# Encoder layer, one core: real-valued position transform inside the second projection, channel transform inside w_in, turned x kept in DRAM, no set-up block

## The chip, the cores and the metric

The kernel runs on one core of one Trainium2 chip. The metric is the device time of one execution in microseconds (us). The kernel before took 4788.79 us, median of three runs (4778.67 to 4791.86). The execution whose trace is read here took 4788.77 us, with a span of 4787.0 us from its first to its last instruction.

## The reference, cut to what matters

One encoder layer is applied to two sequences of 4096 and 2048 positions, 6144 rows of 1024 channels together, all in float32. One projection of RMSNorm(x) gives the queries, keys and values of 12 heads, two gates, and the 256 channels `u` of a Fourier branch:

```
h = rmsnorm(x, norm_g)
proj = h @ w_in
q, k, v, g_attn, u, g_four = split(proj)
q, k = rmsnorm per head
attn = merge of three dilated windowed attentions * silu(g_attn)
uf = u.reshape(B, S, 4, 64)
mixed = fftn(uf, axes=(1, 3), norm="ortho").real
four = einsum('bsgc,gce->bsge', mixed, w_four) * silu(g_four)
return x + concat[attn, four] @ w_out
```

`mixed` is the real part of a two-dimensional transform over the positions and the 64 channels of a group. `w_four` follows as a 64 x 64 matrix for each group. Since `u` is real, the spectrum over the channels of a group is symmetric: 33 cosine and 31 sine sums hold all of it.

## The kernel before, in words

Engines are programmed with semaphores; each engine and each DMA queue works its own list in order, and a block ends when all of its engines have ended. The rows are worked in 48 tiles of 128. There are six blocks, one after the other.

**setup** (L162) loads the constants, multiplies a one-hot table with `rel_bias` (L199, four products into `line`) and folds `w_four` into the channel transform (L203, into `chan_w`).

**project** (L218) runs twice. In each run 1792 columns of `w_in` come in 16 units through six staging buffers (L329); ScalarE rounds each unit into `w_hi` (L476) and VectorE takes the rest into `w_lo` (L596), so that a product of float32 values is three products of rounded ones (L381). A tile has four banks of results, `ps[0]` to `ps[3]`, in the order 3, 0, 1, 2: three of 512 columns and bank 3 of 256, so 72 products of 512 columns and 24 of 256. Ahead of them x is loaded (L318), normalised (`norm_x`), turned by eight TensorE transposes (`turn`, L368, between bank 3 and bank 0, for the next tile) and split into `h_hi` (L431) and `h_lo` (L527). The first run gives q, k and u. Its u is turned by two more transposes (L388) and multiplied by `chan_w` (L396), and 512 columns per row go to the scratch `ab`. Its GpSimd queue fills the pads of `v` (L302) and then spreads `line` into `skew` tables, DRAM to DRAM, by 36 DMAs (L311). The second run loads and turns x again with the kept `rstd_x`, and gives v and the two gates; a gate's silu is an exponential on ScalarE (L454) and three operations on VectorE (L556, L558, L564). Both runs go over the tiles in a hardware loop. The end of the second run issues the first loads of the next block (L335 and L636).

**fourier** (L638) does the transform over the positions in two levels, with float32 matrices. Level 1 multiplies by the 64- or 32-point matrix (L726), cosine and sine halves stacked, and stores the scratches `g_a` and `g_b`; level 2 multiplies by the fine matrices (L731) and stores `four`. All its loads and stores are on SyncE's queue (L636, L683, L695), in pieces of 4096 columns; ScalarE and VectorE copy the results out (L744).

**attention** and **combine** follow. Attention begins with loads of q, k, v and `skew`; combine reads `four` and the gates, and multiplies by `w_out` (L1349).

Of the kernel before, what the change touches and what calls it, by code (L numbers as in the profile page):

```python
# [55 lines left out]
PIECE = 8 * BANK  # L56
# [32 lines left out]
def constants():  # L89
# [7 lines left out]
    a = 2 * np.pi * np.outer(np.arange(HD), np.arange(HD)) / HD  # L97
    two = np.eye(2)
    chan = np.concatenate([np.kron(two, np.cos(a)), np.kron(two, np.sin(a))], axis=1)
    out = {"c_ident": np.eye(P), "c_onehot": onehot, "c_chan": chan}  # L100
    for name, s in zip("ab", SEQS):
        n1 = s // N2
        a = 2 * np.pi * np.outer(np.arange(n1), np.arange(n1)) / n1
        c, sn = np.cos(a), np.sin(a)
        out["c_first_" + name] = np.block([[c, -sn], [-sn, -c]])
        n, k1, k2 = np.arange(N2)[:, None, None], np.arange(n1)[None, :, None], np.arange(N2)[None, None, :]
        a = 2 * np.pi * ((n * (k1 + n1 * k2)) % s) / s
        second = np.concatenate([np.cos(a), np.sin(a)], axis=0) / math.sqrt(s * HD)
        out["c_second_" + name] = second.reshape(2 * N2, n1 * N2)
# [19 lines left out]
def build(nc, io):  # L129
    core = Core(nc, io)  # L130
    with core.keep:
        core.ident = core.sb(core.keep, "ident", [P, P])
        core.rstd_x = core.sb(core.keep, "rstd_x", [P, TILES])
        scratch = {"q": [TOKENS, DA], "k": [TOKENS, DA], "v": [TOKENS + 2 * VPAD, VROW], "gate": [TOKENS, D],
                   "ab": [TOKENS, 2 * DF], "four": [TOKENS, DF], "line": [NH, TABLE],
                   "o": [len(DILS), TOKENS, OROW],
                   "g_a": [2 * SEQS[0] // N2, N2 * DF], "g_b": [2 * SEQS[1] // N2, N2 * DF]}
        scratch |= {f"skew{x.dil}": [NH, x.copies] for x in SPREADS}
        core.dram = {k: nc.dram_tensor("scratch_" + k, s, F32, kind="Internal").ap() for k, s in scratch.items()}
        with ExitStack() as tables:  # L140
            core.zero = core.sb(tables, "zero", [P, VW])
            core.chan_w = core.sb(tables, "chan_w", [P, 2, 2 * P])
            core.line = core.sb(tables, "line", [NH, TABLE])
            setup(core)
            project(core, 0)

        with ExitStack() as spectrum:
            core.four_in = core.sb(spectrum, "four_in0", [P, PIECE])
            core.four_first = {n: core.sb(spectrum, "four_first_" + n, [2 * seq // N2, 2 * seq // N2])
                               for n, seq in zip("ab", SEQS)}  # L150
            core.four_in_loaded, core.four_table_in = core.sem("four_loaded0"), core.sem("four_table_in")
            project(core, 1)
            fourier(core)
# [8 lines left out]
def setup(core):  # L162

    nc, io, dram = core.nc, core.io, core.dram
    loaded, cleared, mm_done = (core.sem("setup_" + n) for n in ("loaded", "cleared", "mm_done"))
    with ExitStack() as st:
        onehot = core.sb(st, "onehot", [BUCKETS + 1, TABLE])
        rel = core.sb(st, "rel", [BUCKETS + 1, NH])
        line = core.line
        chan = core.sb(st, "chan", [P, 2 * P])  # L170
        wf = core.sb(st, "wf", [P, 2, P])
        ps_line = [core.ps(st, f"ps_line{i}") for i in range(-(-TABLE // BANK))]
        ps_chan = [core.ps(st, f"ps_chan{i}") for i in range(2)]
        block = st.enter_context(nc.Block())
        n_loads = 4 + NG

        @block.gpsimd
        def _(pool):
            pool.memset(wf[:], 0.0).then_inc(cleared, 1)
            pool.memset(rel[:], 1.0).then_inc(cleared, 1)  # L180
            pool.memset(core.zero[:], 0.0).then_inc(cleared, 1)

        @block.sync
        def _(sp):
            sp.dma_start(core.ident[:], io["c_ident"]).then_inc(loaded, 16)
            sp.dma_start(onehot[:], io["c_onehot"]).then_inc(loaded, 16)
            sp.dma_start(chan[:], io["c_chan"]).then_inc(loaded, 16)
            sp.wait_ge(cleared, 3)
            sp.dma_start(rel[0:BUCKETS, :], io["rel_bias"]).then_inc(loaded, 16)
            for g in range(NG):  # L190
                lo = HD * (g % 2)
                sp.dma_start(wf[lo:lo + HD, g // 2, lo:lo + HD], io["w_four"][g]).then_inc(loaded, 16)

        @block.tensor
        def _(pe):
            pe.wait_ge(loaded, 16 * n_loads)
            for i in range(len(ps_line)):
                n = min(BANK, TABLE - i * BANK)
                pe.matmul(ps_line[i][0:NH, 0:n], rel[:], onehot[:, i * BANK:i * BANK + n],  # L199
                          start=True, stop=True).then_inc(mm_done, 1)  # L200
            for gp in range(2):
                for ab in range(2):
                    pe.matmul(ps_chan[gp][:, ab * P:(ab + 1) * P], chan[:, ab * P:(ab + 1) * P], wf[:, gp, :],  # L203
                              start=True, stop=True).then_inc(mm_done, 1)

        @block.vector
        def _(dve):
            dve.wait_ge(mm_done, len(ps_line) + 2 * 2)
# [3 lines left out]
            for gp in range(2):  # L212
                dve.tensor_copy(core.chan_w[:, gp, :], ps_chan[gp][:, 0:2 * P])
# [392 lines left out]

class Piece:  # L610


# [874 lines left out]
```

## Time and profile before

| | |
|---|---|
| median of three runs | 4788.79 us (4778.67 to 4791.86) |
| profiled execution, its own time | 4788.77 us |
| its span | 4787.0 us |
| TensorE busy | 4527.7 us (95%) |
| VectorE busy | 2811.1 us (59%) |
| ScalarE busy | 1744.2 us (36%) |
| GpSimd busy | 749.8 us (16%) |
| mean DMA rate | 115 GB/s |

The profile page gives busy time by engine for the whole span, and then the span in 40 slices. Since the blocks follow each other, a block's own length is read from where SyncE issues the first DMA of the next block, and what bounds it is read from the rows of that stretch alone. Matmuls are pipelined: the cost of one is the distance from its start to the start of the next, not its own duration.

### The profile page before, as it was taken

How to read it: one execution, taken by the hardware profiler on the slowest of the kernel's cores; microseconds unless marked ns; L12 is line 12 of the kernel's file. 1: busy time of each engine (PE TensorE's matmuls, PEld its weight loads, DVE VectorE, ACT ScalarE, POOL GpSimd, SP SyncE). 2: the span in 40 equal slices, each digit the busy share in tenths (PEclk: the TensorE clock that was granted, in tenths of full speed). 3: DMA queues.
4: the chain of work that ended last, by engine and by line, in shares of the span. 5: the costliest groups of instructions: out<-in, count | busy, mean ns of one | idle time of the engine just before them, and what ended most of it. 6: DMA issues, size and time to landing. Idle time of an engine off the chain costs nothing. (4 is left out here: it accounts for less than half of the span.)

```text
span 4787.0 us, 86571 instructions
## 1 busy us (share of the span) xinstructions
PE 4527.7 (95%) x28848; PEld 3805.0 (79%) x28848; DVE 2811.1 (59%) x8424; ACT 1744.2 (36%) x4667; POOL 749.8 (16%) x1494
## 2 busy tenths in 40 slices
PE   3999999998999999998499999999999999899999
PEld 2888888886888888873397988979889798778887
DVE  2555555555655555652265656647566466577776
ACT  2222222223222222211254655546555465533332
POOL 2000000000000000000042433424344243300000
PEclk9999999999999999997799999999999999999999
DMA  7212121214211222219833434434353343466665
GB/s 185 79 66 79 66 79 66 78 73 138 74 69 67 74 74 74 74 61 255 183 101 81 120 87 117 102 81 118 87 119 102 81 118 79 133 234 239 243 241 191
DMA packets 549470, 549.16 MB, mean 115 GB/s; under 512 B 187432, under 2 KB 443304, under 8 KB 547797
## 3 DMA queue, kind: packets, MB, share of 16 engines
q1 hardware_dynamic: 502228, 474.35, 34.1%
q0 software_dynamic: 46976, 71.46, 5.3%
q8 instruction: 144, 2.36, 0.2%
q14 instruction: 122, 0.99, 0.1%
HBM read 344.66 MB, written 211.33 MB: 116 GB/s over the span
## 5 line engine op out<-in xcount | busy, mean ns | idle before, releaser
L381 PE MATMUL p_ps<-p_w_hi,p_h_hi 128*128 128x512 f32 (+1 forms) x3072 | 1155.1, 376 | 55.2 <-DVE p_w_lo L596 49.4
L381 PE MATMUL p_ps<-p_w_hi,p_h_lo 128*128 128x512 f32 (+1 forms) x3072 | 1133.2, 369 | 0.0
L381 PE MATMUL p_ps<-p_w_lo,p_h_hi 128*128 128x512 f32 (+1 forms) x3072 | 1133.0, 369 | 0.0
L1167 ACT ACTIVATE att_p<-att_s_b,att_o 128x256 f32<-128x256 f32 (+2 forms) x1728 | 739.2, 475 | 815.8 <-DVE att_o L1217 792.8
L1112 PE MATMUL att_ps_o<-att_v,att_p_t 128*128 128x130 f32 (+1 forms) x6528 | 943.4, 288 | 46.3 <-DMA att_v<-scratch_v 32.9
L1112 PEld LDWEIGHTS att_ps_o<-att_v,att_p_t 128*128 128x128 f32 (+1 forms) x6528 | 817.1, 192 | 146.8 <-issue 47.8
L381 PEld LDWEIGHTS p_ps<-p_w_hi,p_h_hi 128*128 128x128 f32 x3072 | 582.9, 190 | 162.6 <-DVE p_w_lo L596 46.6
L1035 POOL DMA_DIRECT2D scratch_o<-att_o x864 | 503.5, 587 | 1069.3 <-DVE att_o L1224 1047.6
L381 PEld LDWEIGHTS p_ps<-p_w_hi,p_h_lo 128*128 128x128 f32 x3072 | 583.1, 190 | 104.7
L381 PEld LDWEIGHTS p_ps<-p_w_lo,p_h_hi 128*128 128x128 f32 x3072 | 583.2, 190 | 101.7
L1217 DVE CUSTOM_DVE_ANT_0 att_s_b<-att_ps_s,att_bias 128x256 f32<-128x256 f32 (+2 forms) x1488 | 500.0, 386 | 54.1 <-PE att_ps_s L1084 46.9
L1098 PE MATMUL att_ps_p<-ident,att_p 128*128 128x128 f32 (+1 forms) x3264 | 455.8, 282 | 0.0
L1224 DVE COPY att_o<-att_ps_o 128x260 f32<-128x260 f32 x432 | 184.0, 426 | 435.5 <-PE att_ps_o L1112 434.2
L1098 PEld LDWEIGHTS att_ps_p<-ident,att_p 128*128 128x128 f32 (+1 forms) x3264 | 349.1, 139 | 56.3 <-issue 18.5
L558 DVE RECIPROCAL p_denom<-p_denom 128x256 f32<-128x256 f32 x144 | 329.2, 2286 | 4.9
L431 ACT ACTIVATE p_h_hi<-p_ps_t,p_gain 128x128 fp32r<-128x128 f32 x768 | 208.4, 382 | 208.9 <-PE p_ps_t L368 208.9
L538 DVE TENSOR_REDUCE p_sumsq<-p_squares 128x8 f32<-128x512 f32 x144 | 98.7, 686 | 312.7 <-ACT p_squares L437 312.7
L556 DVE TENSOR_SCALAR p_denom<-p_expo 128x256 f32<-128x256 f32 x144 | 48.1, 334 | 387.8 <-ACT p_expo L454 387.8
L437 ACT ACTIVATE p_squares<-p_ps 128x512 f32<-128x512 f32 x144 | 86.1, 598 | 475.3 <-PE p_ps L381 475.3
L1137 ACT ACTIVATE att_p_t<-att_ps_p 128x512 f32<-128x512 f32 (+2 forms) x528 | 243.1, 478 | 0.8 <-PE att_ps_p L1098 0.2
L527 DVE SCALAR_TENSOR_TENSOR p_h_lo<-p_ps_t,p_gain,p_h_hi 128x128 fp32r<-128x128 f32 x768 | 206.8, 342 | 32.6 <-ACT p_h_hi L431 32.6
L1140 DVE COPY att_p_t<-att_ps_p 128x512 f32<-128x512 f32 x288 | 197.5, 686 | 4.0 <-PE att_ps_p L1098 3.4
(158 smaller groups left out, 5930.5 us busy)
## 6 DMA issues: line engine op xcount, KB each, us to landing
att_v<-scratch_v SPq DMA_DIRECT2D x1056, 65.0 KB
scratch_o<-att_o POOLq DMA_DIRECT2D x864, 66.0 KB, 2.7
out_o<-scratch_o SPq DMA_DIRECT2D x144, 396.0 KB, 5.5
p_x<-x SPq DMA_DIRECT2D x96, 512.0 KB, 4.5
scratch_gate<-p_gate SPq DMA_DIRECT2D x48, 512.0 KB, 3.5
out_gate<-scratch_gate SPq DMA_DIRECT2D x48, 512.0 KB, 6.3
out_x<-x SPq DMA_DIRECT2D x48, 512.0 KB, 4.9
y<-out_y SPq DMA_DIRECT2D x48, 512.0 KB, 3.0
```

What stands on the lines that cost most here:

```text
L381: ins = pe.matmul(ps[c][:, 0:width[c]], a[s][:, k, :], b[:, k, cols], start=(k == 0 and n == 0), stop=(k == KC - 1 and n == 2))
L431: ins = act.activation(h_hi[s][:, 4 * j + k, :], ps_t[2 * s + j][:, k * P:(k + 1) * P], ACT.Copy, scale=gain[:, 4 * j + k:4 * j + k + 1])
L527: ins = dve.scalar_tensor_tensor(h_lo[s][:, kk, :], ps_t[2 * s + j][:, k * P:(k + 1) * P], gain[:, kk:kk + 1], h_hi[s][:, kk, :].bitcast(F32),
L558: dve.reciprocal(denom[:, w], denom[:, w]).then_inc(chain, 1)
L1035: pool.dma_start(to, o[u % O][:, t, :]).then_inc(stored[u % O], 16)
L1098: ins = pe.transpose(ps_p[t][0:n, (2 * e + j) * P:(2 * e + j + 1) * P], p[u % 2][:, t, e, first:first + n], core.ident[:])
L1112: ins = pe.matmul(ps_o[:, col:col + 2 * VW], p_t[u % 2][0:n, t, e, j, :], v[u % V][0:n, unit.chunk(at, part), e * VW:(e + 2) * VW], start= ...
L1137: copy = (lambda to, src: engine.activation(to, src, ACT.Copy)) if t == 0 else engine.tensor_copy
L1140: copy(p_t[u % 2][:, t], src).then_inc(p_copied[t], 1)
L1167: act.activation(p[u % 2][:, t, e, 0:at.w], s_b[u % 2][:, t, e, 0:at.w], ACT.Exp, bias=o[u % O][:, t, PAIR_V + e:PAIR_V + e + 1], scale=-1 ...
L1217: dve.tensor_tensor_reduce(at.view(s_b[u % 2][:, t, e, :]), at.view(ps_s[2 * t + e][:, 0:2 * P]), at.bias(bias[b][:, e, :]), -1.0, -3 * NE ...
L1224: dve.tensor_copy(o[u % O][:, :, 0:PAIR_V], ps_o[:, 0:2 * PAIR_V].rearrange("p (t c) -> p t c", t=2)).then_inc(o_copied, 1)
```

## The change

There is no set-up block, and no Fourier block. What they did stands in the two projections, which are now two functions.

`project_first` turns the 256 columns of `w_in` that make u, multiplies them by a 64-point real channel matrix (`turn_w` and `mix_w`: 16 transposes and 16 float32 products of 128 columns), and splits the outcome into `w_hi` and `w_lo`. So the projection gives the channel spectrum itself, 256 real columns, and `turn_u` and `channel_dft` go. Banks run in the order 0, 1, 2, 3. It also stores each tile's `h_hi` and `h_lo` to a new scratch `ht`, 1 MB a tile, behind the load of x on SyncE's queue; the next write of the same buffer waits for that store.

`project_second` loads `h_hi` and `h_lo` from `ht` in place of x: no normalising, no turning, no splitting. Its tile loop is written out, not a hardware loop. Ahead of tile 1 it makes `line` and four small `mix` matrices (four one-hot products and eight float32 products), then the GpSimd queue issues the pads, two loads, and the 36 `skew` DMAs. From tile 3 on, TensorE runs one of 76 jobs behind the first 512-column bank and one behind the last bank of a tile, until tile 40: 24 `first` (two float32 products of 264 and 248 columns), 26 `second` (four of 128 columns, fewer in the last groups) and 26 `mix` (four of 128 columns). ScalarE copies each result out behind its gate work. The loads and stores of the jobs are on the GpSimd queue. The fine tables (3.2 MB) are loaded on SyncE's queue once the weights are split, into the space of the staging buffers.

Cut to its core, the diff is:

```diff
-            setup(core)
-            project(core, 0)
-            project(core, 1)
-            fourier(core)
+        project_first(core)
+        project_second(core)
...
+            def turn_w(r):
+                pe.wait_ge(w_in[r], 16)
...
+                        ins = pe.transpose(ps[2 + r % 2][:, at:at + P], stage[r][:, k, j * P:(j + 1) * P], core.ident[:])
...
+            def mix_w(r):
+                pe.wait_ge(u_copied, r + 1)
...
+                    ins = pe.matmul(ps_t[2 + r % 2][:, i * P:(i + 1) * P], u_t[r % 2][:, i * P:(i + 1) * P], chan[:],
+                                    start=True, stop=True)
...
-                    if half == 0 and n == (3 if first(t) else 1):
-                        turn_u(t)
-                    if half == 0 and n == (3 if first(t) else 2):
-                        channel_dft(t)
...
+                sp.wait_ge(lo_done, t * 2 + 2)
+                sp.dma_start(dram["ht"][bass.ds(t * HT, P), :],
+                             h_hi[s][:].rearrange("p k c -> p (k c)").bitcast(F32)).then_inc(h_stored[s], 16)
+                sp.dma_start(dram["ht"][bass.ds(t * HT + P, P), :],
+                             h_lo[s][:].rearrange("p k c -> p (k c)").bitcast(F32)).then_inc(h_stored[s], 16)
...
+            def load_h(t):
+                s = t % 2
+                if t >= 2:
+                    sp.wait_ge(mm_done[order[-1]], t - 1)
+                for part, to in enumerate((h_hi, h_lo)):
+                    row = t * HT + part * P
...
+            load_h(1)
+            sp.wait_ge(line_copied, LINES)
+            sp.dma_start(dram["line"], line[0:NH, 0:TABLE]).then_inc(line_out, 16)
+            sp.wait_ge(w_lo_done, len(units))
+            for wave in WAVES:
+                at = table_at[wave.name]
+                sp.dma_start(shared[:, at:at + (wave.slots + 1) * P], io["c_second_" + wave.name]).then_inc(table_in, 16)
+            for t in range(TILES):
+                s = t % 2
+                if t + 2 < TILES:
+                    load_h(t + 2)
...
+            load_first(0)
+            load_first(1)
+            pool.wait_ge(line_out, 16)
+            for at, x in zip(TABLE_AT, SPREADS):
...
+                    pool.dma_start(to, src).then_inc(skew_out, 16)
+            for nr in range(n_pieces):
+                store_first(nr)
+                if nr + 2 < n_pieces:
+                    load_first(nr + 2)
+            for s in range(2):
+                pool.wait_ge(g_stored[s], 16 * (n_pieces // 2))
+            load_second(0)
+            load_second(1)
...
+            for t in range(1, TILES):
...
+                for n, c in enumerate(order):
+                    if n == 0:
+                        pe.wait_ge(h_in[t % 2], 32 * (t // 2 + 1))
+                    product(t, c)
+                    if (t, n) in job_at:
+                        work(job_at[t, n])
```

## Rows read from the trace of the kernel before

**Rows 1.** The profile page: span, TensorE's busy time, clock granted in 40 slices.

```profile
span 4787.0 us, 86571 instructions
...
PE 4527.7 (95%) x28848; PEld 3805.0 (79%) x28848; DVE 2811.1 (59%) x8424; ACT 1744.2 (36%) x4667; POOL 749.8 (16%) x1494
...

```

**Rows 2.** By block: start:end, length, busy PE PEld DVE ACT POOL, clock, DMA, GB/s.

```profile
0.00:17.66 17.66, 8.05 (x16) 2.73 (x16) 2.83 (x6) 0.00 (x0) 0.65 (x7) 1.00 0.11 28
17.66:1142.21 1124.55, 1054.19 (x5280) 883.93 (x5280) 607.46 (x2032) 297.31 (x834) 25.65 (x41) 0.99 0.26 85
1142.21:2154.20 1011.99, 989.01 (x4992) 830.63 (x4992) 595.43 (x880) 222.63 (x641) 1.54 (x2) 0.99 0.24 80
2154.20:2339.64 185.44, 131.60 (x320) 55.61 (x320) 37.11 (x56) 31.76 (x56) 0.00 (x0) 0.77 1.03 244
2339.64:4787.00 2447.36, 2344.89 (x18240) 2032.12 (x18240) 1568.23 (x5450) 1192.53 (x3136) 721.98 (x1445) 0.97 0.48 134
```

**Rows 3.** TensorE by time between second projection and Fourier: start, length, line, idle before.

```profile
2144.29 0.40 PE L381 MATMUL p_ps<-p_w_hi,p_h_lo 128*128 128x512 f32 x1
2154.38 6.03 PE L726 MATMUL four_ps<-four_in,four_first_a 128*128 128x512 f32 x10 [9.69 <-PEq L270]
```

**Rows 4.** TensorE by time, one steady tile of the second projection.

```profile
1919.75 0.28 PE L381 MATMUL p_ps<-p_w_hi,p_h_hi 128*128 128x256 f32 x1
...
1922.60 1.04 PE L368 MATMUL p_ps_t<-ident,p_h 128*128 128x128 f32 x8
...
1923.70 0.39 PE L381 MATMUL p_ps<-p_w_lo,p_h_hi 128*128 128x512 f32 x1
...
1940.27 0.28 PE L381 MATMUL p_ps<-p_w_hi,p_h_hi 128*128 128x256 f32 x1
```

**Rows 5.** SyncE's stores of q, two tiles apart, in the first projection.

```profile
901.43 0.33 SPq L345 DMA_DIRECT2D scratch_q<-p_qk  x1
...
944.61 0.33 SPq L345 DMA_DIRECT2D scratch_q<-p_qk  x1
```

**Rows 6.** TensorE by time: the channel transform inside a steady tile.

```profile
1106.82 1.02 PE L396 MATMUL p_ps<-chan_w,p_ut 128*128 128x256 f32 x4
...
1107.91 0.40 PE L381 MATMUL p_ps<-p_w_lo,p_h_hi 128*128 128x512 f32 x1
```

**Rows 7.** TensorE by time: the first projection's longest early wait, and where tile 1 starts.

```profile
51.34 0.58 PE L381 MATMUL p_ps<-p_w_hi,p_h_hi 128*128 128x256 f32 x1 [15.86 <-DVE p_w_lo L596]
...
117.91 0.55 PE L381 MATMUL p_ps<-p_w_hi,p_h_hi 128*128 128x256 f32 x1 [2.37 <-DVE p_ab L585]
```

**Rows 8.** Columns as in rows 2: three stretches, loading weights with and without skew copies.

```profile
30.00:45.00 15.00, 1.62 (x6) 1.35 (x6) 2.85 (x9) 1.96 (x7) 13.32 (x23) 1.00 1.08 105
...
80.00:105.00 25.00, 15.90 (x48) 11.71 (x48) 9.62 (x8) 8.86 (x9) 0.00 (x0) 0.86 1.01 298
1157.00:1168.00 11.00, 11.00 (x53) 9.11 (x53) 8.68 (x8) 7.43 (x7) 0.00 (x0) 0.99 1.05 381
```

**Rows 9.** DMA issues from 18 to 130 us: count, KB each, median us to landing.

```profile
p_x<-x SPq DMA_DIRECT2D x3, 512.0 KB, 20.8
```

**Rows 10.** TensorE by time: 16 small float32 products in attention.

```profile
2388.03 1.95 PE L1112 MATMUL att_ps_o<-att_v,att_p_t 128*128 128x130 f32 x16
```

**Rows 11.** TensorE by time: the second projection's start, tile 0 and tile 1.

```profile
1152.10 0.55 PE L381 MATMUL p_ps<-p_w_hi,p_h_hi 128*128 128x256 f32 x1 [3.34 <-DVE p_w_lo L596]
...
1179.51 0.36 PE L381 MATMUL p_ps<-p_w_hi,p_h_hi 128*128 128x256 f32 x1 [3.50 <-DVE p_gate L564]
```

**Rows 12.** TensorE by time: the one-hot products in the set-up.

```profile
6.48 6.04 PE L199 MATMUL ps_line<-onehot,rel 33*12 33x512 f32 x8 [6.48 <-DMA wf<-w_four]
```

**Rows 13.** DMA issues of the whole span: count, KB each, median us to landing.

```profile
scratch_o<-att_o POOLq DMA_DIRECT2D x864, 66.0 KB, 2.7
...
four_in<-scratch_g_a SPq DMA_DIRECT2D x8, 1024.0 KB, 19.9
```

More of the change, by code:

```diff
@@ L55 @@
 N2 = 64
-PIECE = 8 * BANK
+COS = HD + 2
 def t5_bucket(rel):
@@ L103, in constants @@
         a = 2 * np.pi * np.outer(np.arange(n1), np.arange(n1)) / n1
         c, sn = np.cos(a), np.sin(a)
[L105 to L109, printed above, removed]
+        copies = np.eye(P // n1)
@@ L157, in build, with project_first @@
         combine(core)
[L162 removed]
+U_COLS = slice(3 * BANK, 3 * BANK + DF)
+HT = 2 * P
+def project_first(core):
     nc, io, dram = core.nc, core.io, core.dram
[L165 to L208, printed above, removed]
[L209 to L213 removed]
@@ new lines, in _, with __init__ @@
+            copy_u(3)
+            split_u(2)
+            split_u(3)
+            split(0, 0)
+            for n in range(PARTS, len(units)):
+                if n == 2 * PARTS + 2:
+                    norm_x(1, 1, X_LINKS)
+                split_w(n)
+            tiles(dve, step)
+class Wave:
+    def __init__(self, name, seq, base):
+        self.name, self.seq, self.base = name, seq, base
+        self.n1 = seq // N2
+        self.copies = P // self.n1
+        self.pieces = N2 // self.copies // 4
+        self.slots = self.n1 // 2
+        self.groups = [list(range(k, min(k + 4, self.slots))) for k in range(1, self.slots, 4)] + [[0]]
@@ new lines, with __init__, wave_jobs @@
+WAVES = [Wave(*at) for at in zip("ab", SEQS, BASES)]
+class Job:
+    def __init__(self, kind, wave, piece, part, slots=()):
+        self.kind, self.wave, self.piece, self.part, self.slots = kind, wave, piece, part, slots
+def wave_jobs():
+    jobs, nr, groups = [], 0, []
+    for wave in WAVES:
+        for i in range(wave.pieces):
+            jobs += [Job("first", wave, (nr, i), part) for part in range(2)]
+            nr += 1
+    for wave in WAVES:
+        groups += [(wave, slots) for slots in wave.groups]
+    mixes = lambda n: ([Job("mix", groups[n][0], n, i, groups[n][1][i:i + 2]) for i in range(0, len(groups[n][1]), 2)])
+    for n, (wave, slots) in enumerate(groups):
+        jobs += [Job("second", wave, n, j, slots) for j in ([0] if slots == [0] else [0, 1])]
+        if n >= 1:
+            jobs += mixes(n - 1)
+    return jobs + mixes(len(groups) - 1), groups, nr
```

757 lines of the change are left out of this document (459 added, 298 removed).

## The prediction, made before the result was known

> **What bounds the kernel now.** I read the page first, then the blocks one by one, then single tiles. The page says that TensorE is busy for 95% of the span and that its granted clock is low only in slices 18 and 19 [rows 1]. By block [rows 2]: set-up 17.7 us, first projection 1124.6, second 1012.0, Fourier 185.4, attention with combine 2447.4. In the Fourier block the DMA share is 1.03 and TensorE is busy for 131.6 of 185.4 us at a mean clock of 0.77: that block is bound by transfers, while in both projections the DMA share is about 0.25. So there is room beside the projections for what the Fourier block moves, if TensorE can take its products.
>
> In a steady tile of the second projection TensorE has no gap; the tile takes 1940.27 - 1919.75 = 20.52 us [rows 4], in the first projection 43.18 / 2 = 21.59 us [rows 5]. Here every instruction taken from TensorE is time gained, and every one added is time lost. The starts are another matter: in the first projection TensorE waits for weights, once for 15.9 us, and tile 1 starts only at 117.91, which is 100.3 us after its block began [rows 7]; in the second it starts at 1179.51, after 37.3 us [rows 11]. The difference is what the DMA engines do meanwhile: between 30 and 45 us, with pads and skew copies in flight, they are full and move 105 GB/s, later, with the skew copies, 298, and in the second start, without them, 381 [rows 8].
>
> **Fourier block and set-up.** Both blocks vanish. From where SyncE begins the Fourier block to where it begins attention is 185.4 us [rows 2], and the hand-over that remains (last product at 2144.29, next block's at 2154.38 [rows 3]) is counted with the projection. The set-up's 17.7 us go as well: the first projection's queue starts near 0.7 us.
>
> **First projection, steady tiles.** Two transposes and four products of 256 columns leave each tile. The four take 1107.91 - 1106.82 = 1.09 us less the 0.23 of the product between, 0.86 [rows 6]. All together are the difference between the two projections' tiles, 21.59 - 20.52 = 1.07 us [rows 4, 5]. So a tile is 20.52 us, bound by TensorE as in the second projection now. The new stores to `ht` add 1 MB a tile, 51 GB/s on a queue whose block mean is 85 of at least 298 [rows 2, 8]: hidden, and each has a whole tile before its buffer is written again. They stand behind the load of x and ahead of the stores of q, k and `ab`, which have that tile too.
>
> **First projection, start.** The skew copies and pads leave this stretch, the weight fold enters it. I walk it from the block's start: the first 256-column unit is in SBUF by 6 us; TensorE turns it, VectorE copies, TensorE multiplies, ScalarE and VectorE split, four rounds whose TensorE part is about 3 us each at the low pace of a cold start, so the fold ends near 20 us. The turning of x and its split follow (6 us), the first product stands at about 26 us. From there 12 units of 6 products, at 0.233 us (71 of them from 1923.70 to 1940.27 [rows 4]), make 16.8 us, the cold pace of the first ones and a wait of about 2 us for the second x make 4, and bank 3 is 2.9: tile 1 starts near 49.5 us. The weights no longer decide, since without skew copies they come at 381 GB/s [rows 8], a 0.5 MB unit in 1.4 us. Bounds: 42 us if the fold's rounds overlap fully; 100 us if the start stays as slow as it was [rows 7]. I take 49.5, near the second projection's 37.3 [rows 11] plus the fold. Then 47 tiles, the last without transposes: 49.5 + 47 x 20.52 - 0.9 = 1013; hand-over 7. The second block starts at 1020 instead of 1142.2, **122 us earlier**: 17 of the set-up, 51 of the tiles, 54 of the start.
>
> **Second projection, steady tiles.** Eight transposes go. They and the slower first product behind them reach from 1922.60 to 1923.70, 1.10 us, less 0.23 for the product, 0.87 [rows 4]: a tile is 19.65 us. VectorE and ScalarE lose the splits and the norm. The jobs come back to TensorE. A `first` job has 512 columns in float32, as many as the two channel products of 256: 0.86 us [rows 6]. `second` and `mix` jobs have 8 instructions of 128 columns, at 1.95 / 16 = 0.122 us each [rows 10] 0.98 us; the short groups less. Sum: 24 x 0.86 + 52 x 0.95 = 70 us. Bounds: 65 (all at the 0.86), and 148 (1.95 for each), if changing between the two kinds of products drained the array each time; rows 6 show such a change inside a tile without that loss, so I take 70. Their waits (results copied out three jobs before, pieces loaded two pieces before) lie a tile or more back: hidden by 20 us of products. Without that cover a piece would show a store and a load, 2 x 2.7 us [rows 13] or more. ScalarE's added copies come behind its gate work and have the next tile before their bank is needed.
>
> **Second projection, start.** h comes from DRAM, so the first product comes about 2 us sooner than 1152.10. Eleven small loads amid the weights cost about as much. So tile 0 ends about 32 us from the block's start, an estimate from rows 11 (37.3 less the 3.5 of the wait there, less 2). Then come the one-hot products, 6.04 us at the cold pace [rows 12], 3.0 warm; a wait for VectorE, which has the last gate and two copies ahead, 3.8 us (it is the 3.50 of rows 11, later); and 16 instructions of the small matrices, 2.0. Tile 1 starts at 40.8, was 37.3.
>
> **What the moved DMAs do there.** SyncE now queues the 3.2 MB of fine tables ahead of the h of tile 2, while pads and skew copies fill the GpSimd queue. Needed is that h at the end of tile 1, 60.5 us after the block's start. How the two queues share is shown for the first start alone: an x of 0.5 MB then took 20.8 us to land [rows 9], 25 GB/s. Between that and all of the 298 GB/s of rows 8 I take half, 149. 4.2 MB at 149 GB/s, from about 41 us, is there after 28 us, at 69; with 60 GB/s during the pads' last 10 us it is 72. The stall is 8 to 12 us; I take 11. Bounds: nothing (381 GB/s, all for SyncE), and 52 us (nothing until skew is done). The skew copies last some 100 us from tile 0's end, and the second pair of pieces behind them is needed about 10 us later: nothing, up to 30. Between the last `first` and the first `second` job lie a copy-out, a store and a load, by estimate some 12 us (two landings of 2.7 to 4, issues, the copy) against 9.5 of products: 3 us once. The Trainium skill, "DMA: Bandwidth & Descriptors", Queues, rings and completion order, says that an engine goes round the queues packet by packet; by that rule each queue gets about half, which is 149 here and a stall of 8 us, and the slow x of rows 9 disagrees in part. The skill's "SBUF — State Buffer", section on the DVE-blocks-DMA trap, speaks against moving DMAs to the GpSimd queue: VectorE's copies can hold up the writing of their descriptors. No row here shows it; it would add a few us to the 3.
>
> Block length to attention's start: 40.8 + 11 + 3 + 47 x 19.65 + 70 + hand-over 9.9 = 1058, against 1012.0: **46 us longer**.
>
> **Sum.** 1020 + 1058 + 2447 = 4525 us of span; with the 1.8 outside it (4788.77 less 4787.0) **4527 us**. The profiled execution is at the median of the runs (4788.77 and 4788.79), so nothing is to be shifted. A difference of 0.3%, 14 us, is about what a measurement of this kernel can tell from none.
>
> **The rivals.** First, the moved copies starve the second projection: SyncE gets nothing until the skew copies are done, h of tile 2 comes 52 us late instead of 11, pieces wait 20 more: 4527 + 61 = 4588. For it: the x that took 20.8 us. Against: rows 8, where weights still came beside skew. Second, the start of the first projection does not shorten, because the fold's chain takes the place of the skew wait: 4527 + 51 = 4578. Against it: 37.3 us without skew. Third, **slower than before**: the jobs stand in TensorE's own list, so each waits in place; if round trips on the GpSimd queue were as in the full Fourier block, where a load took 19.9 us [rows 13], and no tile hid them, store and load of each of 26 pieces and groups would cost 40 us, 26 x 40 = 1040. It decides from 262 / 26 = 10.1 us uncovered a piece; then the time is 4789 and above, at 12 us 4839. Against: the DMA share of 0.25, where 2.7 us is the landing. Fourth, that the copies disturb nothing and the fold overlaps: 4527 - 11 - 7 = 4509.
>
> **Chances.** Forecast 0.62, first rival 0.17, second 0.08, third 0.03, fourth 0.10. The forecast's own range is 4510 to 4555; with the fourth and most of the first two, **4500 to 4590**. Faster by over 0.3%: 0.96; within 0.3%: 0.01; slower: 0.03.
>
> **What would show it.** Attention should start at 2078 instead of 2339.64, with its own length unchanged. Tiles of 20.5 us in the first projection and 19.65 plus two jobs in the second; tile 1 of the first near 50 us; one wait for h at tile 2 of the second and one before the first `second` job, none longer than 15 us. Wrong would be: waits of TensorE for pieces in most tiles, a job far above 1 us, or tile 1 of the first projection after 70 us.

## The result, and the profile after

The changed kernel takes 4523.57 us, median of four runs (4521.0 to 4526.32); the kernel before, beside it, 4790.32 (4778.67 to 4796.84). The ratio is 0.9448, with a 95% interval of 0.943 to 0.9466: 267 us or 5.5% faster. The prediction was 4527, from 4500 to 4590. The profiled execution took 4521.0 us, with a span of 4519.2, 1.8 us outside it as before.

The page of the changed kernel, with the clock line of the page before ahead of it: TensorE is busy for 96%, and the dip that the Fourier block made in its clock (the two slices with a 7; 0.77 in [rows 2]) is gone.

```profile
PEclk9999999999999999997799999999999999999999
```

```profile
span 4519.2 us, 84021 instructions
...
PE 4347.2 (96%) x28408; PEld 3725.0 (82%) x28408; DVE 2586.4 (57%) x7796; ACT 1672.6 (37%) x4375; POOL 824.7 (18%) x1596
...
PEclk9999999998999999998999999999999999899999
```

By block, with the columns of [rows 2]: first projection, second projection, attention with combine.

```profile
0.00:1013.02 1013.02, 995.40 (x5040) 835.01 (x5040) 544.79 (x1892) 310.11 (x882) 0.21 (x5) 1.00 0.36 126
1013.02:2077.33 1064.31, 1010.81 (x5128) 863.14 (x5128) 473.05 (x454) 169.97 (x357) 102.47 (x148) 0.97 0.45 138
2077.33:4519.20 2441.87, 2341.00 (x18240) 2026.86 (x18240) 1568.59 (x5450) 1192.56 (x3136) 721.99 (x1445) 0.97 0.48 134
```

Set-up and Fourier block, 203.1 us together, are gone; the first projection is 111.5 us shorter, the second 52.3 longer, attention with combine 5.5 shorter. Attention and combine have the same code in all the kernels here, and in the seven that also leave its addresses as the changed kernel has them these two took from 2441.9 to 2451.2 us; so those 5.5 us can't be told from what these two move by themselves, and below, where an effect is smaller than 10 us, blocks and tiles are compared, not whole times. An experiment for which no ratio is given was executed once.

TensorE at the start of the first projection and of its tile 1 (compare [rows 7]):

```profile
14.26 1.16 PE L305 MATMUL p_ps_t<-p_chan,p_u_t 128*128 128x128 f32 x8 [0.68 <-DVE p_u_t L481]
...
22.21 0.77 PE L329 MATMUL p_ps<-p_w_hi,p_h_hi 128*128 128x512 f32 x1 [4.28 <-DVE p_w_lo L492]
...
44.82 0.40 PE L329 MATMUL p_ps<-p_w_hi,p_h_hi 128*128 128x512 f32 x1
...
65.33 0.40 PE L329 MATMUL p_ps<-p_w_hi,p_h_hi 128*128 128x512 f32 x1
```

TensorE's part of the fold ends at 15.4, tile 1 starts at 44.82 instead of 117.91, and a tile takes 20.51 us. In the second projection, all waits of TensorE above 3 us, and the one-hot products (compare [rows 11]):

```profile
1020.33 0.58 PE L757 MATMUL p_ps<-p_w_hi,p_h_hi 128*128 128x256 f32 x1 [12.40 <-DVE p_w_lo L931]
...
1047.36 3.12 PE L813 MATMUL p_ps_f<-p_f_have,p_rel 33*12 33x512 f32 x8
1058.36 3.78 PE L818 MATMUL p_ps_f<-p_f_end 128*128 128x128 f32 x16 [7.88 <-DVE p_f_mid L943]
...
1091.74 0.58 PE L757 MATMUL p_ps<-p_w_hi,p_h_hi 128*128 128x256 f32 x1 [9.82 <-DMA p_h_lo<-scratch_ht]
...
1169.99 1.22 PE L769 MATMUL p_ps_f<-p_f_have,p_first_a_c 128*128 128x264 f32 x2 [5.92 <-DMA p_f_have<-scratch_ab]
...
1391.95 2.05 PE L785 MATMUL p_ps_f<-p_shared,p_f_have 128*128 128x128 f32 x8 [8.92 <-issue]
```

These are the start of the block; the wait for VectorE ahead of the small matrices; the h of tile 2; a piece; and the first `second` job. ("issue" says that the trace names nothing that ended the last wait; the kernel's text points to the load of that job's piece, and one experiment tests it.) After 1392 TensorE does not wait again in this block. The starts of tiles there: a tile with two `first` jobs (21.00 us), one with a `second` and a `mix` job (21.03), one without (19.22; [rows 4] showed 20.52 with transposes and without jobs):

```profile
1332.35 0.46 PE L757 MATMUL p_ps<-p_w_hi,p_h_hi 128*128 128x256 f32 x1
...
1353.35 0.46 PE L757 MATMUL p_ps<-p_w_hi,p_h_hi 128*128 128x256 f32 x1
...
1512.57 0.36 PE L757 MATMUL p_ps<-p_w_hi,p_h_hi 128*128 128x256 f32 x1
...
1533.60 0.36 PE L757 MATMUL p_ps<-p_w_hi,p_h_hi 128*128 128x256 f32 x1
...
1990.81 0.28 PE L757 MATMUL p_ps<-p_w_hi,p_h_hi 128*128 128x256 f32 x1
...
2010.03 0.28 PE L757 MATMUL p_ps<-p_w_hi,p_h_hi 128*128 128x256 f32 x1
```

So the total was close to the forecast, but not by the forecast's terms: four waits were larger than predicted or not predicted, and the tile was 0.43 us shorter than predicted, 47 times. The experiments ask what made the first start short, what each wait stands for, and where the 0.43 us come from.

### The profile page after: what moved, and what is told of

It reads as the page before. It is cut to its first block and busy times, and to the rows that moved or that the text cites. A ratio compares the mean times of both kernels' runs of the same rounds, so it can differ in the third digit from the quotient of the medians.

```text
span 4519.2 us, 84021 instructions
## 1 busy us (share of the span) xinstructions
PE 4347.2 (96%) x28408; PEld 3725.0 (82%) x28408; DVE 2586.4 (57%) x7796; ACT 1672.6 (37%) x4375; POOL 824.7 (18%) x1596
## 5 line engine op out<-in xcount | busy, mean ns | idle before, releaser
L757 PE MATMUL p_ps<-p_w_hi,p_h_hi 128*128 128x512 f32 (+1 forms) x1536 | 572.0, 372 | 26.4 <-DVE p_w_lo L931 16.6
L329 PE MATMUL p_ps<-p_w_hi,p_h_hi 128*128 128x512 f32 (+1 forms) x1536 | 568.4, 370 | 4.3 <-DVE p_w_lo L492 4.3
```

Source lines behind the costliest of these rows:

```text
L329: ins = pe.matmul(ps[c][:, 0:width[c]], a[s][:, k, :], b[:, k, cols], start=(k == 0 and n == 0), stop=(k == KC - 1 and n == 2))
L757: ins = pe.matmul(ps[c][:, 0:width[c]], a[s][:, k, :], b[:, k, cols], start=(k == 0 and n == 0), stop=(k == KC - 1 and n == 2))
```

## Experiments

### The copies at the first start, in the kernel before

```diff
+                pool.wait_ge(mm_done[order[-1]], 3)
                 for row in (0, P, VPAD + TOKENS, VPAD + TOKENS + P):
...
```

> The kernel before, with one thing changed: the GpSimd queue issues the pads and the 36 skew copies only when tile 2 of the first projection is done, instead of at its start. Theory (the copies made that start slow, the step of the prediction that gave 54 us): tile 1 starts some 37 to 42 us after its block begins, as in the second projection, instead of 100.3; near 57 instead of 117.91; the total is 55 to 63 us shorter, near 4730, and the copies cost nothing in the steady tiles. Rival (the start is bound by the weights or by the chain of splits anyway): tile 1 stays later than 90 and the total moves by less than 15 us.

Measured: 4753.22 us, a ratio of 0.993 (0.9914 to 0.9947) to the kernel before. TensorE at tile 1, and later at tile 4; and the DMA engines between (last three columns: clock, DMA share, GB/s):

```profile
61.80 0.55 PE L382 MATMUL p_ps<-p_w_hi,p_h_hi 128*128 128x256 f32 x1 [2.37 <-DVE p_ab L586]
...
149.82 0.47 PE L369 MATMUL p_ps_t<-ident,p_h 128*128 128x128 f32 x1 [17.70 <-DVE p_h L520]
```

```profile
120.00:140.00 20.00, 12.12 (x65) 10.19 (x63) 4.07 (x11) 0.81 (x2) 13.16 (x23) 0.89 1.03 130
```

Tile 1 starts 56.1 us sooner. That is the step of the prediction, shown by itself: the pads and skew copies (moved together here), not the weights or the splits, made that start slow. The second half of the theory was wrong: 23 us come back in tiles 4 to 6, where TensorE waits for the h of a tile whose x is loaded while pads and copies hold the engines (1.03 of their time for 130 GB/s). So 31 us are gained, not the 55 to 63 expected: the steady tiles do not hide these transfers for free.

### Who makes the h of tile 2 late: pads, skew copies or tables

In the changed kernel the GpSimd queue issues the pads from 1048, and DMA goes on like this (columns of [rows 2]):

```profile
1045.00:1050.00 5.00, 5.00 (x18) 2.25 (x17) 3.97 (x6) 2.21 (x5) 1.93 (x2) 1.00 0.02 5
1050.00:1072.00 22.00, 14.12 (x72) 12.53 (x71) 12.23 (x14) 1.58 (x3) 4.40 (x5) 0.77 1.10 91
1072.00:1092.00 20.00, 10.18 (x45) 8.15 (x44) 6.94 (x6) 1.26 (x3) 15.94 (x27) 0.88 0.99 338
```

For 22 us the engines are full at 91 GB/s. By queue, first from 1060 to 1070 and then from 1072 to 1092 (packets, MB, share of the engines; q0 is GpSimd's queue, q1 holds SyncE's):

```profile
q0 software_dynamic: 279, 0.64, 105.2%
q1 hardware_dynamic: 2, 0.01, 1.5%
```

```profile
q1 hardware_dynamic: 1113, 6.04, 85.2%
q0 software_dynamic: 1506, 0.70, 13.7%
```

Beside the pads SyncE's queue gets nearly nothing; beside the skew copies it gets nearly all. SyncE issues `line` at 1059.23 and the h at 1060.67; the GpSimd queue, which waits for `line` to land, goes on only at 1076.06, after 16.8 us:

```profile
1048.07 4.69 POOL L628 DMA_DIRECT2D scratch_v<-p_zero  x4 [33.13 <-PE p_ps L757]
1051.94 2.46 POOL L641 DMA_DIRECT2D p_f_have<-scratch_ab  x2
1076.06 21.07 POOL L681 DMA_DIRECT2D scratch_skew<-scratch_line  x36 [21.66 <-DMA scratch_line<-p_f_mid]
```

Four kernels move one of the parts each. First the pads, to the end of the GpSimd queue's list; then the skew copies, to the same place:

```diff
-            for row in (0, P, VPAD + TOKENS, VPAD + TOKENS + P):
...
+            for row in (0, P, VPAD + TOKENS, VPAD + TOKENS + P):
...
             for s in range(2):
                 pool.wait_ge(four_stored[s], four_stores(len(mixes) + (len(mixes) + s) % 2))
```

> The changed kernel, with the four pad stores issued last on the GpSimd queue instead of first. Theory P (the pads alone hold the DMA engines from 1050 to 1072, at 66 to 107 GB/s, and line, tables and the h of tile 2 stand behind them): line lands within 5 us of its issue instead of 17, the skew copies begin near 1062 instead of 1076, the wait for h at tile 2 falls from 9.8 to 0 to 4 us, the wait of 5.9 us for a piece goes, since skew ends 14 us sooner; the block is 15 to 22 us shorter. Theory S (the skew copies take what h needs, as the prediction had it): the h wait stays at 8 to 15 us, since the skew copies now begin together with the tables.

```diff
-            pool.wait_ge(line_out, 16)
-            for at, x in zip(TABLE_AT, SPREADS):
...
+            pool.wait_ge(line_out, 16)
+            for at, x in zip(TABLE_AT, SPREADS):
...
             for s in range(2):
                 pool.wait_ge(four_stored[s], four_stores(len(mixes) + (len(mixes) + s) % 2))
```

> The changed kernel, with the 36 skew copies issued last on the GpSimd queue, behind the last mix store, instead of ahead of the first pieces. Theory P (the pads cause the h wait): it stays at 6 to 10 us, since the pads still hold the engines until 1072; the piece wait of 5.9 us goes. Theory S (the skew copies cause it): the h wait falls under 3 us. By either the piece wait at the third piece is gone, 9 us of the block with its slow pace behind it. The copies end before the last tile (some 100 us of copying against 7 tiles without jobs, 135 us), so attention does not wait for them.

Then the tables, behind the h of tile 4; and the pads where they were, but from a wide zero tile:

```diff
-            for wave in WAVES:
...
             for t in range(TILES):
...
+                if t == 2:
+                    for wave in WAVES:
...
```

> The changed kernel, with the fine tables (3.2 MB on SyncE's queue) loaded behind the h of tile 4 instead of ahead of the h of tile 2. Theory T (the bytes of the tables ahead of h are what makes it late): the h wait goes from 9.8 to 0, since 1 MB instead of 4.2 stands behind the pads, and the block is 11 to 14 us shorter. Rival (h is late because of the other queue, whatever stands ahead of it on its own): the wait stays above 6 us. The first second-level job, at tile 15, does not wait for the tables by either.

```diff
-        rel, zero = sb("rel", [BUCKETS + 1, NH]), sb("zero", [P, VW])
+        rel, zero = sb("rel", [BUCKETS + 1, NH]), sb("zero", [P, VROW])
...
-                               zero[:].rearrange("p (h w) -> p h w", h=1).broadcast_to([P, NH + 1, VW])
...
+                pool.dma_start(dram["v"][row:row + P, :], zero[:]).then_inc(pads_out, 16)
```

> The changed kernel, with the four pad stores read from a zero tile as wide as a row of v (845 floats in one piece) instead of 13 repeats of 65 floats; same place on the queue, same bytes. Theory W (the pads are slow because their source comes in pieces of 260 bytes): the DMA engines are free again within 8 us of the first pad, line lands before 1066 instead of 1076, the h wait at tile 2 falls from 9.8 to 0 to 4 us, the piece wait of 5.9 goes or halves, the block is 12 to 20 us shorter. Rival (four stores of 0.43 MB on this queue hold the engines some 20 us whatever their pieces): line lands after 1072, and both waits stay within 3 us of what they were.

Measured, in us (the block is from the first load of h to attention's first load):

| kernel | `line` issued, skew begins | h wait, tile 2 | piece wait | block |
|---|---|---|---|---|
| after | 1059.23, 1076.06 | 9.8 | 5.9 | 1064.3 |
| late_pads | 1059.42, 1066.49 | 3.1 | none | 1046.6 |
| late_skew | moved | 12.4 | none | 1057.1 |
| late_tables | 1060.89, 1076.94 | none | 15.0 | 1059.8 |
| wide_pads | 1058.79, 1064.69 | 1.8 | none | 1043.8 |

The waits of TensorE by what it waited for (us in total, times, longest): late_skew, then late_tables, then wide_pads.

```profile
PE p_ps L757 <- DMA p_h_lo<-scratch_ht: 12.4, 1, 12.4
```

```profile
PE p_ps_f L771 <- DMA p_f_have<-scratch_ab: 15.0, 1, 15.0
```

```profile
PE p_ps L755 <- DMA p_h_lo<-scratch_ht: 1.8, 1, 1.8
```

Theory S, the nearest to the prediction, falls: without the skew copies the wait is there all the same. (At 12.4 us it is longer than the 6 to 10 that theory P gave it; why, was not tried.) The pads are one half of the cause. The 2.0 MB that 91 GB/s make in 22 us are the pads' 1.7 (four times 128 rows of 3380 bytes) and little more. The 4.2 MB of tables and h behind them are the other half: with the tables later the wait is gone too. That saves only 4.5 us, not the 11 to 14 expected, because the piece behind the skew copies lands about when it landed (TensorE's first product with it starts at 1167.24, before at 1169.99), and TensorE, now earlier, waits 15.0 us for it. `wide_pads` shows what is wrong with the pads: the same bytes from one run of 3380 bytes a row instead of 13 of 260 hold the engines for a shorter time, `line` lands in 5.9 us instead of 16.8, and the block is 20.6 us shorter. The Trainium skill, "DMA: Bandwidth & Descriptors", Specifications, gives 512 bytes as the least size for full rate; the trace agrees in direction, 91 GB/s in the stretch with the pieces of 260, though no run tries sizes between 260 and 3380.

### The mix products and the change between jobs

```diff
+    gap = lambda j: 0 if jobs[j].kind == "first" else 1
-    job_at = {(BEGIN + j // 2, 1 + 2 * (j % 2)): j for j in range(len(jobs))}
+    job_at = {(BEGIN + gap(j) + j // 2, 1 + 2 * (j % 2)): j for j in range(len(jobs))}
...
-            pe.wait_ge(line_copied, 2)
-            for j in range(2):
...
             for t in range(1, TILES):
+                if t == 2:
+                    pe.wait_ge(line_copied, 2)
+                    for j in range(2):
...
+                if t == 1:
                     for j in range(2):
                         dve.wait_ge(mix_mm, j + 1)
```

> The changed kernel with two places moved: the eight products of the small mix matrices stand behind tile 1 instead of ahead of it, and all second and mix jobs stand one tile later, so that the tile behind the last first job has no job. Theory: the wait of 7.9 us ahead of the mix products and the 8.9 us ahead of the first second-level job both go, with the slow pace behind each; tile 1 starts 9 to 11 us sooner (but the h wait at tile 2 grows by as much, since that h lands when it landed), tile 15 and 16 together are 12 us shorter; the block is 12 to 15 us shorter in all. Rival (the waits are for something else: DMA time that a tile does not cover): the tile without job is followed by a wait above 3 us.

Measured: tile 1 starts at 1050.39, 11.4 us sooner; the h of tile 2 is waited for 21.4 us instead of 9.8, as its landing did not move (1093.02, before 1091.74); tile 15, now empty, takes 19.39 and tile 16 20.95, where tile 15 took 33.05 before; the block is 12.1 us shorter. The theory holds, and the first of its two moves shows that a wait taken away in front of another is worth nothing by itself. Why 8.7 us of products were no cover for the first `second` job stands on the GpSimd queue of the changed kernel:

```profile
1375.75 0.69 POOL L649 DMA_DIRECT2D scratch_g_b<-p_f_mid  x1 [20.31 <-ACT p_f_mid L863]
1387.01 2.51 POOL L660 DMA_DIRECT2D p_f_have<-scratch_g_a  x4 [10.58 <-DMA scratch_g_b<-p_f_mid]
```

The store takes 11.3 us to land, and the loads behind it are there 4.9 us after their issue began. Of the 12 stores on that line none landed in under 10.7 us:

```profile
DMA to landing us min/median/max: 10.7/15.9/33.3
```

### Where the short tile comes from

The 512-column products of the changed second projection start 0.227 us apart; everywhere else, before and after, 0.233. This was not predicted. Two explanations were open: its tile loop is written out, and its operands lie at other addresses. In each partition of SBUF its h and w both begin at 640 past a multiple of 1024 bytes; in the first projection h begins 32 bytes past a place that agrees with w modulo 128, in combine m begins 64 past one. The first test brings both to a multiple of 128, by a wider gain in the first projection and a filler ahead of acc in combine; the second puts a filler ahead of h_hi in both projections. (The number in a filler is of floats, 4 bytes each.)

```diff
-        gain = sb("gain", [P, KC])
+        gain = sb("gain", [P, 4 * KC])
...
+        sb("apart", [P, 16])
         acc, term = sb("acc", [P, DA]), [sb(f"term{i}", [P, DA]) for i in range(2)]
```

> The changed kernel, with nothing but SBUF addresses moved: 96 bytes behind gain in the first projection (h_hi and h_lo then begin at a multiple of 128 bytes, before at 32 past one) and 64 bytes ahead of acc in combine (m_hi and m_lo, before at 64 past one). Theory A (the pace of 0.227 us in the changed second projection comes from the address: it alone has both operands at multiples of 128): the 512-column products of the first projection and of combine go from 0.2333 to 0.227 us, a tile of the first projection from 20.51 to about 20.1, combine 12 to 15 us shorter, the total 30 to 37 us shorter. Theory L (it comes from the tile loop being written out, not a hardware loop): nothing moves, within 3 us.

```diff
+        sb("apart", [P, 8])
         h_hi = [sb(f"h_hi{i}", [P, KC, P], F32R) for i in range(2)]
```

> The changed kernel with h_hi and h_lo 32 bytes further on in both projections: from a multiple of 128 to 32 past one in the second, from 32 to 64 past one in the first. Theory A (address): the second projection's products go from 0.227 to 0.2333 us, its tile without jobs from 19.22 to 19.65, the block 20 us longer; the first projection tells whether 64 is enough (0.227 there) or not (0.2333). Theory L (the loop written out): the second projection stays at 0.227 and 19.22.

Measured: `aligned` 4518.9 us (4509.21 to 4523.96), ratio to before 0.9436 (0.9421 to 0.9451), not to be told from the changed kernel; its first projection's tile takes 20.43 us, late in the block, instead of 20.51. Theory A in that form falls: a multiple of 128 is not enough. But `shifted` makes theory L fall too: the loop is written out as before, and the tile without jobs takes 19.64 us, the block 1084.2, 19.9 longer.

```profile
2022.81 0.28 PE L759 MATMUL p_ps<-p_w_hi,p_h_hi 128*128 128x256 f32 x1
...
2042.45 0.28 PE L759 MATMUL p_ps<-p_w_hi,p_h_hi 128*128 128x256 f32 x1
```

So a new theory: what counts is where the two operands of a product lie against each other, h or m, which is loaded into TensorE and stays there (the stationary operand), and w, which streams past it (the moving one). Fillers stand ahead of h_hi in the first projection, ahead of h_hi in the second, and ahead of acc in combine.

```diff
+        sb("apart", [P, 120])
...
+        sb("apart", [P, 32])
...
+        sb("apart", [P, 48])
```

> The changed kernel with only SBUF addresses moved. In the changed kernel h_hi, h_lo, w_hi and w_lo of the second projection all begin at 640 past a multiple of 1024 bytes, and that block alone runs at 0.227 us a product. Here the first projection and combine get the same (480 bytes ahead of h_hi, 192 ahead of m_hi's group), and the second projection's h is moved 128 bytes further. Theory R (what counts is that stationary and moving operand begin at the same place modulo 1024): the first projection goes from 0.2333 to 0.227 us, 20.51 to 20.1 a tile, combine too; the second projection goes to 0.232 or more. Theory M (a multiple of 128 is enough, and in the first projection and combine something else, such as their transposes or the work of ScalarE and VectorE, holds the pace): those two stay at 0.232 to 0.2333, and the second projection stays at 0.227, 19.22 a tile without jobs.

A tile of the first projection, 20.13 us, and one of the second without jobs, 19.58; then the products of combine in 550 us, the changed kernel's count (2183) and that of `residue` (2231):

```profile
807.01 0.28 PE L330 MATMUL p_ps<-p_w_hi,p_h_hi 128*128 128x256 f32 x1
...
827.14 0.28 PE L330 MATMUL p_ps<-p_w_hi,p_h_hi 128*128 128x256 f32 x1
...
2007.78 0.28 PE L759 MATMUL p_ps<-p_w_hi,p_h_hi 128*128 128x256 f32 x1
...
2027.36 0.28 PE L759 MATMUL p_ps<-p_w_hi,p_h_hi 128*128 128x256 f32 x1
```

```profile
3950.00:4500.00 550.00, 521.06 (x2183) 405.06 (x2182) 1.00 0.66 236
```

```profile
3950.00:4500.00 550.00, 520.18 (x2231) 416.48 (x2232) 1.00 0.67 239
```

All three places moved as theory R says, one of them to the worse. Which modulus it is, the last of these asks, with other widths in the same three places:

```diff
+        sb("apart", [P, 184])
...
+        sb("apart", [P, 128])
...
+        sb("apart", [P, 112])
```

> The changed kernel with only addresses moved: h of the first projection and m of combine 256 bytes past the place that the moving operand has modulo 1024, h of the second projection 512 bytes past it. The chunks of h are 512 bytes apart and those of w 7168, so half the products of a good placement already stand 512 off; so 512 should change nothing: the second projection stays at 0.227 us and 19.22 a tile. If the rule is modulo 512, the first projection is at 20.4 a tile and 0.232 us a product; if it is modulo 256, it is at 20.13 and 0.2275, and combine too.

Measured: the first projection is at 20.13 us a tile, the second at 19.22, and the products of combine start 0.227 us apart, as in `residue`.

```profile
907.81 0.28 PE L330 MATMUL p_ps<-p_w_hi,p_h_hi 128*128 128x256 f32 x1
...
927.93 0.28 PE L330 MATMUL p_ps<-p_w_hi,p_h_hi 128*128 128x256 f32 x1
```

Distances of 0, 256 and 512 bytes between the two are alike; 128 costs 0.30 to 0.36 us a tile (first projection 20.43, second 19.58), 32 costs 0.38 and 0.42 (20.51, 19.64), 64 costs 0.26 (20.39). What in the chip does this, the runs do not show. Nor do they show that it is the distance: only h and m were moved, and the moving operands begin at the same place modulo 256 in all blocks of the changed kernel and its variants, so the place of the stationary operand alone would give the same list. A run that moves w is missing.

### All of it

All four waits are taken away (pads last, skew copies two behind each piece and then one behind each mix store, tables behind the h of tile 4, mix products behind tile 1, an empty tile between the jobs), and the addresses are those of `aligned`. The edits are those shown above, but for the skew copies:

```diff
                 if nr + 2 < n_pieces:
                     load_first(nr + 2)
+                if nr == 0:
+                    pool.wait_ge(line_out, 16)
+                skew(2 * nr)
+                skew(2 * nr + 1)
...
                     store_mix(mixes.index(j))
+                    k = 2 * n_pieces + mixes.index(j)
+                    if k < NH * len(DILS):
+                        skew(k)
```

> All of it at once: the addresses of the aligned kernel, pads last on the GpSimd queue, skew copies two at a time behind the pieces and one behind each mix store, fine tables behind the h of tile 4, mix products behind tile 1, an empty tile between the two kinds of jobs. If each of the causes is the one named, the four waits in the second projection (h 9.8, piece 5.9, transition 8.9, mix matrices 7.9, with the slow pace behind them some 43 us) go, and with the addresses 30 to 37 us more: 4521 - 43 - 33 = 4445, from 4435 to 4465. If the addresses do nothing: 4470 to 4490.

Measured: 4476.37 us (4473.91 to 4485.89), ratio to before 0.9359 (0.9347 to 0.9372). The second projection is 42.4 us shorter, 43 were expected, and its only waits are those of the first products; the 33 us expected of the addresses were missing, as `aligned` had shown.

```profile
1009.92:2031.86 1021.94, 1001.90 (x5128) 856.41 (x5128) 473.05 (x454) 169.81 (x357) 103.12 (x147) 0.99 0.45 143
```

Then the same with two of the fillers of `residue` in place of those of `aligned`, and the second projection's h where the changed kernel has it:

```diff
+        sb("apart", [P, 120])
...
+        sb("apart", [P, 48])
```

> The kernel with the four waits of the second projection taken away (as in the run with all of it), and the addresses of the residue run for the first projection and combine, with the second projection's left as in the changed kernel: stationary and moving operands at the same place modulo 1024 in all three. Against the 4476.4 of the run with all of it: the first projection 14.5 us shorter (1009.9 to 995.4, as the residue run had it), combine 48 tiles of 48 products of 0.2323 to 0.2273 us, 11.5 us; 4450, from 4440 to 4460. If the address gain were given back by a later wait, 4470 or more.

Measured: 4447.93 us (4442.23 to 4454.31), ratio to before 0.9291 (0.9278 to 0.9304); it beats both kernels, the changed one by 76 us. First projection 994.2, second 1022.3, attention with combine 2429.6:

```profile
0.00:994.24 994.24, 976.45 (x5040) 835.08 (x5040) 544.32 (x1892) 309.78 (x882) 0.21 (x5) 1.00 0.37 128
994.24:2016.54 1022.30, 1001.96 (x5128) 856.64 (x5128) 472.71 (x454) 170.01 (x357) 103.25 (x147) 0.99 0.45 143
2016.54:4446.10 2429.56, 2329.39 (x18240) 2030.19 (x18240) 1568.45 (x5450) 1192.61 (x3136) 723.09 (x1445) 0.97 0.49 135
```

## Why the prediction was right, and where only its total was

| term of the sum | predicted | measured |
|---|---|---|
| second block starts | 1020 | 1013.0 |
| its tile 1 starts, after | 40.8 | 48.8 |
| h of tile 2, with the slow pace ahead of it and behind it | 11 | 13.3 |
| a piece behind the skew copies | 0 (up to 30) | 9.0 |
| first `second` job | 3 | 12.0 |
| 47 tiles | 923.6 | 903.3 |
| jobs | 70 | 68 |
| hand-over | 9.9 | 9.6 |
| attention and combine | 2447 | 2441.9 |
| sum, span | 4525 | 4519.2 |

**Set-up and Fourier block** went as predicted, and attention starts at 2077.33 for a predicted 2078.

**First projection.** The steady tile is right (20.51 for 20.52), and with it the claim that the stores of `ht` are hidden. The start was predicted for the right reason, which the first experiment shows; its size was off by 4.7 us, since the four rounds of the fold end at 15.4 and not near 20: they overlap nearly as the lower bound had it. Another 2 us come from the tiles and the hand-over. (Of the 54 us that the prediction puts down to the start, its own figures give 100.3 less 49.5, which is 50.8; the rest is the end of the block. Measured, 100.3 became 44.8, which is 55.4 less.)

**Second projection, tiles and jobs.** Taking 0.87 us for the eight transposes was right: with h 32 bytes off, as far as the projections before have it, the tile is 19.64 for a predicted 19.65. The further 0.42 us come from where the change happened to put h, a term that the prediction did not have. The jobs cost 0.89 (`first`) and 0.905 us each, 68 in all; changing between the kinds of products costs nothing, as [rows 6] said.

**Its start.** The prediction took the wait for VectorE from [rows 11], 3.5 us, and put one gate and two copies ahead of it. There TensorE waited for the first gate alone and had products to do while the others were worked off; here VectorE, busy with weights until 1045.6, had the silu of all three banks to do from 1046.1 to 1057.1, and then the two copies: 7.9 us. The products of the small matrices ran at the low clock, 3.4 us for 2.0, and tile 0 ended at 34.3 for 32.

**h of tile 2.** The mechanism was wrong, and the size came out by luck. The prediction gave SyncE's queue 60 GB/s beside the pads and then, beside the skew copies, half of 298. In the trace it got 0.01 MB from 1060 to 1070, beside the pads, and 6.04 of 6.76 MB from 1072 to 1092, beside the skew copies. h was there 78.7 us after the block's start and not 72, but the end of tile 1, which needs it, was late as well, at 68.9 for 60.5: so the wait is 9.8 for 11. The bound of 52 us, which the first rival uses, does not come out of the prediction's figures: copies of some 100 us from 32 on end at 132, 72 after 60.5. The Trainium skill, "DMA: Bandwidth & Descriptors", Queues, rings and completion order, has each engine go round its queues packet by packet; 279 packets of one queue against 2 of the other from 1060 to 1070, and the 16.8 us of `line`, do not agree with half a share each. The clue stood in [rows 8]: 105 GB/s with the engines full was put down to pads and skew copies together, but without skew copies the pads do the same.

**The piece and the first `second` job.** "Hidden by 20 us of products" was right for 24 of 26 pieces and groups, and wrong where the queue was not in its steady state. For the change of jobs the step took a landing of 2.7 to 4 us from [rows 13]; this queue's stores of g took 10.7 to 33.3. The other row of the group, 19.9 us, in place of one landing would have made the chain some 28 us and the stall some 19, which is too much: the store took 11.3 us and the load 4.9. The third rival's round trips were there, too: store and load took more than its limit of 10.1 us a piece, and it failed only because a tile of products covers them. Whether VectorE's copies have a part in these landings was not tried.

**What was missing altogether** is the clock behind a wait. After 5.9 us without products the granted clock was at half for the next ones, and that tile took 3.0 us more than its wait and the 21.0 of its products:

```profile
1166.00:1170.00 4.00, 0.01 (x1) 0.04 (x1) 0.00 (x0) 0.00 (x0) 0.00 (x0) 0.89 0.42 152
1170.00:1175.00 5.00, 5.00 (x12) 3.96 (x13) 0.00 (x0) 0.66 (x2) 0.00 (x0) 0.50 0.15 54
1175.00:1180.00 5.00, 5.00 (x22) 4.08 (x21) 0.00 (x0) 0.57 (x2) 0.00 (x0) 0.91 0.00 0
```

Twelve products in the five microseconds of the second line, 22 in those of the third. The Trainium skill, "TensorE: Matmul & The Clock Gate", What's actually happening, calls the low level the default that activity lifts; these rows agree. Behind the waits at 1091.74 and 1391.95 it was 2.6 and 3.1, and in tile 1, behind the wait for VectorE and the small matrices, 0.9.

So the errors cancelled: -7.0 at the start of the block, +28.3 in the four waits and starts, -20.3 and -2 in tiles and jobs, -5 in attention, which is within what that block moves by itself. **The rivals:** the first (skew starves the block) is refuted by `late_skew`, the second (the start does not shorten) by the first experiment; the third (slower than before) by the total and by tiles of 21 us without a wait; the fourth (the copies disturb nothing, the fold overlaps) by the waits, though its fold came nearly true, 4.7 of its 7 us.

## What to carry to other kernels

A transfer that moves beside steady work is hidden only if its queue is in the steady state there too: look at what holds the DMA engines at the moment of the move (full at a low rate is the sign), and at the landing of stores on that very queue, not of the nicest store in the trace. Charge a wait of TensorE like those here (5.9 to 9.8 us) with the slow pace behind it (2.6 to 3.1 us), and take away the waits of a chain together: one of them alone can be given to the next, as the 11.4 us of tile 1's start were.

## What the runs showed of the hardware

Two things were not expected. Where the stationary operand lies in SBUF set the pace of these streams of products: 0, 256 or 512 bytes from the moving operand's place (modulo 1024), 0.227 us for 512 columns; 32, 64 or 128 past such a place, 0.232 to 0.233. That was worth 16 to 20 us a projection and some 10 in combine, for a few bytes of padding; whether the distance counts or the stationary operand's own place, the runs leave open. And four stores of 0.43 MB from pieces of 260 bytes held all DMA engines for some 20 us, so that a small store on another queue landed after 16.8 us; read from one run a row, they let it land after 5.9.
